# A hybrid retention and stick-breaking block on Trainium2: ScalarE rounds the high parts of six weight pieces, GpSimd only subtracts

## What is computed

```python
z = jnp.einsum('bthd,bshd->bhts', q[:, t0:t1], k[:, :t1]) * scale
log_1m = jnp.where(valid, -jax.nn.softplus(z), 0.0)
log_stick = lax.cumsum(log_1m, axis=3, reverse=True) - log_1m
a = jnp.where(valid, jnp.exp(jax.nn.log_sigmoid(z) + log_stick), 0.0)
outs.append(jnp.einsum('bhts,bshd->bthd', a, v[:, :t1]))
```

## Time and profile before

| what | value |
|---|---|
| median of three runs | 1855.76 us |
| profiled execution, its own time | 1849.14 us |
| its span | 1847.3 us |
| mean granted TensorE clock | 0.978 of full |
| TensorE matmul busy | 1734.9 us (94%) |
| VectorE busy | 928.3 us (50%) |
| GpSimd busy | 640.6 us (35%) |
| ScalarE busy | 543.6 us (29%) |

### The profile page before, as it was taken

How to read it: one execution, slowest core, us unless ns; L and a number is a source line. 1 busy time by engine, 2 the same in 40 slices (tenths; PEclk the granted TensorE clock), 3 DMA queues, 4 the chain that set the end, 5 groups by cost and what they waited for, 6 DMA issues and landing times.

```text
span 1847.3 us, 24815 instructions
## 1 busy us (share of the span) xinstructions
PE 1734.9 (94%) x9648; PEld 1436.4 (78%) x9648; DVE 928.3 (50%) x1291; ACT 543.6 (29%) x928; POOL 640.6 (35%) x272
## 2 busy tenths in 40 slices
PE   2699999989999989999999999889999999999998
PEld 1587777767798979897888899668888888888876
DVE  6646667767445454544111527582543536262516
ACT  3344545501012121211000245423232333333332
POOL 3123124224331313131333554344354453534420
PEclk8699999999999999999999999999999999999999
DMA  8000001136420101110311345120202111111213
GB/s 324 22 24 23 24 23 35 46 132 239 154 83 26 47 27 39 34 46 24 137 46 45 125 160 194 46 69 23 91 22 68 34 57 45 45 57 34 69 57 126
DMA packets 38077, 135.11 MB, mean 73 GB/s; under 512 B 5861, under 2 KB 6757, under 8 KB 37481
## 3 DMA queue, kind: packets, MB, share of 16 engines
q1 hardware_dynamic: 30304, 109.27, 17.7%
q10 hardware_dynamic: 7688, 24.67, 3.6%
HBM read 121.33 MB, written 12.60 MB: 72 GB/s over the span
## 4 chain that ended last, share of the span: by engine, by line
PE 82%; DVE 11%; issue 2%; ACT 2%; DMA 1%; POOL 1%; POOLq 0%; DVEq 0%; SPq 0%; ACTq 0%
PE ps L501 15%; PE ps L503 15%; PE ps L502 15%; PE ps L845 5%; PE ps L847 5%; PE ps L846 5%; PE ps L562 3%; PE ps L563 2%; PE ps L564 2%; PE ps L595 2%; PE ps L579 2%; PE ps L612 2%; PE ps L726 1%; DVE uu L1330 1%; DVE sg L1291 1%
## 5 line engine op out<-in xcount | busy, mean ns | idle before, releaser
L410 POOL TENSOR_TENSOR w_hi<-raw,zero 128x1024 fp32r<-128x1024 f32 x74 | 149.8, 2024 | 740.2 <-PE ps L503 309.2
L501 PE MATMUL ps<-r_hi,w_hi 128*128 128x512 f32 x640 | 252.7, 395 | 2.1 <-issue 2.1
L503 PE MATMUL ps<-r_hi,w_lo 128*128 128x512 f32 x640 | 254.0, 397 | 0.0
L502 PE MATMUL ps<-r_lo,w_hi 128*128 128x512 f32 x640 | 251.9, 394 | 0.0
L501 PE MATMUL ps<-w_hi,a_hi 128*128 128x256 f32 x768 | 222.6, 290 | 16.4 <-DVE qkT L1464 8.9
L503 PE MATMUL ps<-w_hi,a_lo 128*128 128x256 f32 x768 | 218.1, 284 | 0.0
L502 PE MATMUL ps<-w_lo,a_hi 128*128 128x256 f32 x768 | 218.0, 284 | 0.0
L412 POOL TENSOR_TENSOR w_lo<-raw,w_hi 128x1024 fp32r<-128x1024 f32 x74 | 191.5, 2588 | 5.8
L1598 DVE TENSOR_TENSOR m<-m,ps 128x512 f32<-128x512 f32 x224 | 146.3, 684 | 71.1 <-PE ps L847 70.7
L442 POOL TENSOR_TENSOR w_lo<-w,w_hi 128x1024 fp32r<-128x1024 f32 x39 | 99.5, 2552 | 231.2 <-ACT w_hi L1124 231.2
L845 PE MATMUL ps<-w_hi,f_hi 128*128 128x512 f32 x392 | 156.3, 399 | 10.1 <-issue 9.0
(11 more groups left out here) (226 smaller groups left out, 3343.1 us busy)
## 6 DMA issues: line engine op xcount, KB each, us to landing
raw<-wstream SPq DMA_DIRECT2D x112, 512.0 KB, 3.6
ada_r<-ada_rows SPq DMA_DIRECT2D x32, 512.0 KB, 4.9
w<-wstream SPq DMA_DIRECT2D x32, 512.0 KB, 3.6
ada_s<-ada SPq DMA_DIRECT2D x8, 1024.0 KB, 18.5
xs<-x SPq DMA_DIRECT2D x2, 2048.0 KB, 11.2
m_dram<-m1s ACTq DMA_DIRECT2D x1, 4096.0 KB, 16.3
m<-m_dram ACTq DMA_DIRECT2D x1, 4096.0 KB, 12.4
x_dram<-m ACTq DMA_DIRECT2D x8, 512.0 KB, 3.5
```

What stands on the lines that cost most here:

```text
L410: nc.gpsimd.tensor_tensor(w_hi[:, slot, part], raw[:, h, :], zero[:, 0:1].broadcast_to([P, RAW]), ALU.add).then_inc(w_split, 1)
L501: nc.tensor.matmul(outp, lh, rh, start=(k == 0), stop=False)
L502: nc.tensor.matmul(outp, lh, rl, start=False, stop=False)
L503: last = nc.tensor.matmul(outp, ll, rh, start=False, stop=(k == chunks - 1))
```

## The change

For pieces 2 to 7 ScalarE makes the high part of each half with a Copy activation from `raw` to `w_hi` and adds 1 to a new semaphore `stick_whi`. The first half is issued right behind the eviction (`high`) of the last tile that reads the slot, the second half one unit later, behind that unit's sigmoids. GpSimd waits for `stick_whi` only, subtracts, and adds 2 to `w_split` for each half. Pieces 0, 1 and all from 8 on are as before.

```diff
+SLOT_FREE = {TILE_AT["k", 0, 1]: 2, TILE_AT["v", 0, 7]: 3, TILE_AT["k", 1, 1]: 4, TILE_AT["k", 2, 1]: 5, TILE_AT["v", 1, 7]: 6, TILE_AT["k", 3, 1]: 7}
...
             piece(0, 1, 0, TL_STICK)
             piece(1, 2, 1, TL_STICK)
-            for n, last in ((2, ("k", 0, 1)), (3, ("v", 0, 7)), (4, ("k", 1, 1)), (5, ("k", 2, 1)), (6, ("v", 1, 7)), (7, ("k", 3, 1))):
-                piece(n, n + 1, n % 2, TL_STICK + TILE_AT[last] + 1)
+            for n in range(2, PC_GATE + 2):
+                for h in range(2):
+                    part = slice(h * RAW, (h + 1) * RAW)
+                    pool.wait_ge(stick_whi, 2 * (n - 2) + h + 1)
+                    nc.gpsimd.tensor_tensor(w_lo[:, n % 2, part], raw[:, h, :], w_hi[:, n % 2, part].bitcast(f32),
+                                            ALU.subtract).then_inc(w_split, 2)
...
+            def piece_high(n, h):
+
+                act.wait_ge(raw_full[h], 16 * (n + 1))
+                nc.scalar.activation(w_hi[:, n % 2, h * RAW:(h + 1) * RAW], raw[:, h, :], ACT.Copy).then_inc(stick_whi, 1)
+
+            late = None
             high(0)
             high(1)
             for U in range(ALL_UNITS + 3):
...
                         nc.scalar.activation(sg[:, U % 2, h, 0:w], z, ACT.Sigmoid).then_inc(sg_done, 1)
+                if late is not None:
+                    piece_high(late, 1)
+                    late = None
                 for n, _, k1 in STICK_BESIDE.get(U, ()):
                     if k1 == KC:
                         high(n)
+                        if n in SLOT_FREE:
+                            piece_high(SLOT_FREE[n], 0)
+                            late = SLOT_FREE[n]
```

More of the change, by code:

```diff
@@ L284, in build_block @@
         zero_set = sem("zero_set")
-        w_split, out_whi = sem("w_split"), sem("out_whi")
+        w_split, stick_whi, out_whi = sem("w_split"), sem("stick_whi"), sem("out_whi")
         gemm_done = sem("gemm_done")
```

## The result

| | before | changed |
|---|---|---|
| median of seven runs | 1853.19 us | 1843.44 us |
| lowest to highest | 1851.36 to 1860.39 | 1840.80 to 1847.84 |
| profiled execution, its own time | 1849.14 us | 1840.80 us |
| its span | 1847.3 us | 1839.0 us |

The ratio is 0.9945 (95% interval 0.9925 to 0.9965): 0.55% faster, between 0.35% and 0.75%. The forecast was 0.31%. The direction and the mechanism of the forecast hold; its size is too small, and most of the experiments are about what was missing.

The account below looks back on a forecast made before the run. TensorE was taken to bound the kernel, stalled by VectorE's weights behind GpSimd's splits. Terms -6.71 + 0.9 = -5.8 us against the median of 1855.76 gave 1850.0 us (-0.31%), range 1842.5 to 1857.0.

Parts of the forecast that it names:

- The bound and the reachable stall: Stick-breaking stage: TensorE bounds; five of its six waits for VectorE's weights `sg`, 6.71 us, can go.
- Turns by whole instructions: Shared SBUF port: VectorE operations with two SBUF inputs and GpSimd operations lock it for a whole instruction each.
- The partial-gain rival: Pieces 3 and 6 keep up to 1.5 us of each 2.57, piece 2 costs 1.4: -2.3 us, 1853.5; chance 0.14.
- Pieces 4, 5, 7: Their TensorE stalls (0.54, 0.49, 0.54) go, with 1.7 us in hand; gain 0 to 1.57 us, all taken.
- Piece 2: No stall before; its later second half makes TensorE wait 0.4 or 1.4 us, middle 0.9 taken.
- Piece 8's 1.27 us stay; nothing is given back in the `ada` stage: TensorE's wait behind piece 8, untouched, stays 1.27 us; the later `ada_rows` chain moves with TensorE; taken-back rival's chance 0.08.
- The slower rival: Stage: each of 12 ScalarE copies (1.06 us) delays scores, scans and products in full: +6.9 us, 1862.7; chance 0.05.
- The sum: Whole kernel: -6.71 + 0.9 = -5.8 us; against the median of 1855.76, 1850.0 us, -0.31%.
- the two v-type stalls: TensorE's waits at pieces 3 and 6, whose slot a v tile frees: 2.57 us each, both go.
- The chances: Whole kernel: forecast 0.62; faster by over 0.5% 0.10, within 0.5% 0.85, slower by over 0.5% 0.05.
- The rival of a larger gain: End of the stage: piece 8's wait goes too, 1.27 us more: -7.1 us, 1848.7; chance of more than forecast 0.07.
- the sixth stall: TensorE's wait for `sg` before 370.66 us, behind piece 8: 1.27 us, out of the change's reach.

Follow-up runs that it names:

- the first trace: The kernel before, unchanged, in the trace that the prediction rested on: stage 308.37 us.

## Why the prediction was right, and what it missed

- **The bound and the reachable stall** (6.71 us in five waits behind GpSimd's splits): right at full clock. All five are gone, and by the evictions they were 7.04 us.
- **Turns by whole instructions**: right, to 0.1 us in the scans and the product of piece 3. Its chain of times ended with 0.5 us in hand, measured 0.45. The partial-gain rival, which had these stalls staying in part, is out.
- **Pieces 4, 5, 7**: gain 1.79 us for 1.57 forecast. For piece 4 the product ends at 188.95 and TensorE takes it at 190.40, a margin of 1.45 us for 1.7 forecast.
- **Piece 2**: the mechanism was right and the size was off. Two operations were found 0.01 us apart and the middle of the two outcomes, 0.9 us, went into the sum. The product was first (123.62 to 124.84), the low part's record runs from 123.69 to 127.05, and the wait is 1.4 us, the upper bound. A middle of two outcomes is a value that neither gives.
- **Piece 8's 1.27 us stay; nothing is given back in the `ada` stage**: right. TensorE's wait for `m1s` there is 4.6 us in the changed kernel and 5.0 before, and from the end of the stage on the changed kernel's span is the shorter one, by 2.0 us.
- **The slower rival**: out; doubled copies cost 1.5 us, not 12.7.
- **The sum**: -5.8 us forecast, -5.66 us in the stage of the profiled pair. Against the medians it is -9.75. The term that is mis-sized is the price of the two v-type stalls, 2 × 2.57 = 5.1 us. By the evictions across pieces 3 and 6 they cost 5.25 us in the first trace, and 8.9 us on average over the four traces of the kernel before. The step behind it took the profiled execution, 6.6 us faster than the median of its kernel as then known (some 4 us by the seven runs), for a typical one and carried the difference over as a constant. The stage showed a granted clock of 1.00 in the earlier trace rows, and the prediction did not ask what a wait of 2.57 us does to it in another execution. Over the four traces the stage takes 312.1 us on average; over the two of the changed kernel 302.8. That is 9.3 us, against the 9.75. How often the clock fell in the stage in the timed runs themselves is not known, only their mean clock; that it fell as often as in the traces is inferred.
- **What is left to luck**: both traces of the changed kernel are the fastest runs of their timings (1840.80 and 1840.89 us). Outside the stage they take 1536.3 and 1536.2 us, the four before 1539.4 on average. This is no sign of a gain: the six variants in which the clock did not fall in the stage either take 1537.6 to 1545.9 us there.
- **The chances**: 0.85 went to within 0.5%, on the argument that the whole reachable stall was less than 9.3 us. The measured change lies at 0.55% with an interval on both sides of that line, so by its median it is in the 0.10 that was left for faster by over 0.5%. That share was given to the spread of the median; the prediction did not see that part of this spread was the clock in the stalls, which the change removes. The forecast also took 0.5% for what can be told from no change, where the measured interval is 0.2% to either side. The rival of a larger gain was there with 0.07, but with another mechanism (the sixth stall going too), which did not happen.

## What to carry to other kernels

Where GpSimd and VectorE work side by side on SBUF, count GpSimd's work in a row against VectorE's room before its next deadline; moving its high parts to ScalarE, which had gaps, took all five stalls behind these pieces out, for a new one of 1.4 us. A stall of TensorE of some 2.5 us should be priced by several traces, since the clock may fall with it: here that made 2.6 us into 4.1 or 5.5. A stage's length between two fixed instructions, which repeated to 0.2 us where the clock did not fall, shows such a gain better than whole times that spread over 7 us. When a profiled execution is faster than the median, ask which of the waits that you are about to remove went lightly in it.

## What the runs showed of the hardware

- TensorE's granted clock fell from full to half with waits of 2.57 to 2.9 us in 11 of 13 cases (6 of 8 in the kernel before, 2 of 2 with ScalarE's copies for pieces 2, 4, 5 and 7 only, 3 of 3 with GpSimd's high parts at the new places), never with the waits of 0.5 to 1.4 us of this stage, and always, in 14 of 14 traces, with the wait of 4.2 to 5.2 us behind it. In the stage the fall began within the wait or up to 1.6 us after it, and cost some 1.5 or 2.9 us on top.
- The spread of one kernel's times goes with this clock. The seven runs of the changed kernel, by mean granted clock: 0.980 with 1840.8, 1841.0 and 1841.3 us; 0.977 with 1843.4; 0.976 with 1846.2 and 1847.4; 0.974 with 1847.8. Among the nine traces without a fall in the stage, the time outside the stage goes from 1536.2 us at a mean clock of 0.980 to 1545.9 at 0.974.
- A VectorE operation that waits for its turn is recorded as a longer one: the product of 1024 took 1.22 us alone and 3.28 behind a low part of 2.41, while that low part kept its 2.41 when it was first. A copy of 2 columns was held up too, to 1.85 us; undisturbed, in the changed kernel, it took 0.17.
